# The first LayerNorm's parameters and the constants loaded from ScalarE's queue instead of SyncE's

## The reference, cut to what matters

```python
def layer_norm(x, g, b):
    xf = x.astype(jnp.float32)
    mu = jnp.mean(xf, axis=-1, keepdims=True)
    xc = xf - mu
    var = jnp.mean(xc * xc, axis=-1, keepdims=True)
    return (xc * lax.rsqrt(var + LN_EPS) * g + b).astype(x.dtype)

def reference(x, ln0_g, ln0_b, w_in, ...):
    x = layer_norm(x, ln0_g, ln0_b)
    cos, sin = axial_rope_tables(s, x.dtype)
    for l in range(DEPTH):
        h = x @ w_in[l]
        xf, q, k, v, g_f, g_a = jnp.split(h, SPLITS, axis=-1)
        # Fourier branch, attention branch, gates, output projection
        x = layer_norm(DEEPNORM_ALPHA * x + mixed @ w_out[l], ln1_g[l], ln1_b[l])
        y_p = peer_ffn(x, peer_w_query[l], peer_sub_keys[l], peer_u[l], peer_v[l])
        x = layer_norm(DEEPNORM_ALPHA * x + y_p, ln2_g[l], ln2_b[l])
    return x
```

## Time and profile before

| | us |
|---|---|
| median of 3 runs | 3690.21 (3690.01 to 3690.3) |
| the profiled execution | 3692.19 |
| its span in the trace | 3690.0 |
| PE busy | 3648.8 |
| DVE busy | 2554.0 |
| POOL busy | 2544.3 |
| ACT busy | 1271.2 |

### The profile page before, as it was taken

The page is one execution under the profiler, slowest core; times in us unless marked ns, Lnnn a source line. Parts: engine busy times, 40 slices in busy tenths (PEclk is TensorE's granted clock), DMA queues, the critical chain, the costliest instruction groups (busy, mean ns, idle before and its releaser), DMA issues.

```text
span 3690.0 us, 54294 instructions
## 1 busy us (share of the span) xinstructions
PE 3648.8 (99%) x18216; PEld 3006.1 (81%) x18216; DVE 2554.0 (69%) x4735; ACT 1271.2 (34%) x1859; POOL 2544.3 (69%) x1122
## 2 busy tenths in 40 slices
PE   8999999999999999999999999999999999999998
PEld 7778888888888888888887788888888888888886
DVE  7645979966565656677665469799656565657776
ACT  1651134454344434211126412344444334441110
POOL 6445553349999999877764545533599999998775
PEclk9999999999999999999999999999999999999999
DMA  4223247883333333454321222388634333435542
GB/s 155 69 70 106 100 143 226 244 252 114 125 140 133 114 125 141 178 190 185 137 105 69 80 102 105 138 243 248 212 128 150 120 114 129 150 119 185 202 182 102
DMA packets 221243, 537.87 MB, mean 146 GB/s; under 512 B 9408, under 2 KB 140736, under 8 KB 172864
## 3 DMA queue, kind: packets, MB, share of 16 engines
q1 hardware_dynamic: 47968, 337.14, 25.4%
q10 hardware_dynamic: 173152, 199.13, 16.5%
HBM read 437.67 MB, written 98.57 MB: 145 GB/s over the span
## 4 chain that ended last, share of the span: by engine, by line
PE 95%; DVE 2%; POOL 1%; issue 1%; ACT 0%; DMA 0%; DVEq 0%; POOLq 0%; ACTq 0%
PE bank L1592 30%; PE bank L1593 29%; PE bank L1594 29%; PE bank L1921 2%; PE bank L1922 2%; POOL part_l L529 1%; PE bank L1718 1%; PE bank L1881 1%; PE bank L1706 1%; PE bank L1697 0%; PE bank L1698 0%; POOL part_h L541 0%; DVE stats L1038 0%; DVE bank L1054 0%; PE bank L1670 0%
## 5 line engine op out<-in xcount | busy, mean ns | idle before, releaser
L529 POOL TENSOR_TENSOR part_l<-landing,part_h 128x1024 fp32r<-128x1024 f32 x496 | 1285.7, 2597 | 529.3 <-ACT part_h L806 421.2
L1592 PE MATMUL bank<-XTh,part_h 128*128 128x512 f32 (+1 forms) x2688 | 1047.4, 390 | 3.9 <-DVE XTl L1074 2.5
L1593 PE MATMUL bank<-XTl,part_h 128*128 128x512 f32 (+1 forms) x2688 | 1034.1, 385 | 0.0
L1594 PE MATMUL bank<-XTh,part_l 128*128 128x512 f32 (+1 forms) x2688 | 1034.0, 385 | 0.0
L541 POOL TENSOR_SCALAR part_h<-landing 128x1024 fp32r<-128x1024 f32 x244 | 313.4, 1285 | 497.5 <-PE bank L1594 376.0
L575 POOL TENSOR_TENSOR part_l<-vraw,part_h 128x1024 fp32r<-128x1024 f32 x238 | 596.7, 2531 | 68.4 <-ACT part_h L932 68.4
L1592 PEld LDWEIGHTS bank<-XTh,part_h 128*128 128x128 f32 x2688 | 505.2, 188 | 102.7 <-DVE XTl L1074 3.4
L1594 PEld LDWEIGHTS bank<-XTh,part_l 128*128 128x128 f32 x2688 | 505.1, 188 | 101.3
L1593 PEld LDWEIGHTS bank<-XTl,part_h 128*128 128x128 f32 x2688 | 505.6, 188 | 95.9
L1501 DVE TENSOR_TENSOR X<-X,bank 128x512 f32<-128x512 f32 x544 | 345.0, 680 | 87.3 <-PE bank L1594 87.3
L932 ACT CAST part_h<-vraw 128x1024 fp32r<-128x1024 f32 x238 | 242.1, 1045 | 340.7 <-POOL vraw L582 280.5
(11 more groups left out here) (222 smaller groups left out, 6168.5 us busy)
## 6 DMA issues: line engine op xcount, KB each, us to landing
landing<-stream SPq DMA_DIRECT2D x248, 1024.0 KB, 4.8
vraw<-stream SPq DMA_DIRECT2D x68, 1024.0 KB, 6.5
dense_gates<-spill ACTq DMA_DIRECT2D x32, 2048.0 KB, 9.2
gate<-dense_gates ACTq DMA_DIRECT2D x62, 1024.0 KB, 4.8
early_acts<-early ACTq DMA_DIRECT2D x112, 256.0 KB, 2.2
acts_in<-early_acts ACTq DMA_DIRECT2D x28, 1024.0 KB, 7.5
LNP<-ln ACTq DMA_DIRECT2D x4, 1024.0 KB, 4.8
X<-x SPq DMA_DIRECT2D x4, 512.0 KB, 7.3
```

Source lines behind the costliest of these rows:

```text
L529: nc.gpsimd.tensor_tensor(halves(part_l[s], h), halves(landing[s], h), halves(part_h[s], h).bitcast(F32), ALU.subtract).then_inc(split.sem, 1)
L1592: nc.tensor.matmul(dst, sth, mvh, start=first, stop=False)
L1593: nc.tensor.matmul(dst, sth, mvl, start=False, stop=False)
L1594: return nc.tensor.matmul(dst, stl, mvh, start=False, stop=last)
```

## The change

Two transfers leave SP's queue and are issued by ACT as the first thing in its program, `LNP` before `C`. Their sources, targets and semaphores stay as they were, and so does everything that waits for them. What is left on SP's queue in the beginning is X 0, X 1, `landing[0]`, X 2, X 3, `landing[1]`.

```diff
@@ -443,11 +443,7 @@
             for s in range(LANDINGS):
                 for tb in (2 * s, 2 * s + 1):
                     sp.dma_start(X[:, tb, :], x[tb * P:(tb + 1) * P]).then_inc(x_in[tb], 16)
-                if s == 0:
-                    sp.dma_start(LNP[:], ln0.partition_broadcast(P)).then_inc(ln_in.sem, 16)
                 sp.dma_start(landing[s][:], flat[s]).then_inc(landed[s], 16)
-                if s == 0:
-                    sp.dma_start(C[:], consts).then_inc(const_in, 16)
 
             def rounds(first, end, ahead):
                 with sp.Fori(first, end) as r:
@@ -639,6 +635,8 @@
                     nc.scalar.copy(XTh[:, 4 * h:4 * h + 4, tb * P:(tb + 1) * P],
                                    bank[banks[i]][:].rearrange("p (k t) -> p k t", k=4)).then_inc(xt_high.sem, 1)
 
+            act.dma_start(LNP[:], ln0.partition_broadcast(P)).then_inc(ln_in.sem, 16)
+            act.dma_start(C[:], consts).then_inc(const_in, 16)
             for k in range(2):
                 act.sem_inc(spilled[k].sem, 16)
             root(1, slice(0, 2))
```

## The result

| | before | after |
|---|---|---|
| median of 22 runs, us | 3690.58 | 3695.53 |
| profiled execution, us | 3692.19 | 3696.05 |
| its span, us | 3690.0 | 3694.2 |

The ratio is 1.0014, with a 95% interval of 1.0008 to 1.0020: 5.0 us slower, clear of zero and within the 0.2% that the forecast called no difference. One of the 22 runs of the kernel before took 4818 us; without it the median is 3690.55, and the ratio leaves it out. Lines from 446 on have lower numbers now (1605 is 1603, 1064 is 1062, 1066 is 1064, 1592 is 1590).

What follows compares the result with a forecast made beforehand. PE, busy 3648.8 of 3690.0 us, was taken as the bound, the start being set by DVE's chain to the second pair. That pair's delay, +3.4 to +4.0, taken as +3.7, gave 3690.2+3.7 = 3693.9 us; range 3689.6 to 3696.2.

Steps and rivals of the forecast that it cites:

- no difference: Whole kernel: the forecast shift, +3.7 us, is half of the 0.2% (7.4 us) a measurement can tell; chance of same 0.95.
- pairwise sharing: Start transfers: both queues share by packets, X 0 with LNP, X 1 with C; 3693.9, own range 3692.9 to 3694.9, chance 0.47.
- the signs that the prediction named: X 1 after 8 us, C before 10, DMA wait, four steps over 1.28, second pair at 29 to 31, entry 35.5 to 37.5.
- Issue time is worth nothing: First issues: SP's sooner by 1.1 us or so, ACT's table load moved behind its issues; neither gains anything.
- Order of arrival: Start transfers: X 0 at 7.02, X 1 at 9.50, landing[0] at 11.97; X 1 late by 2.5 to 3.7 us.
- the mild rival: Start transfers: a head start puts X 1 ahead of most of LNP; +2.2 us, 3692.4, chance 0.28.
- Turns with POOL: First pair: all four DVE steps alternate with POOL; fourth ends at 22.95 (POOL first) or 20.9 (DVE first), before 16.54.
- Second pair: DVE's second pair of token blocks: begins at 30.9 with POOL first, 4.0 us later than before; some loss comes back.
- Downstream: From POOL's end and XTl to PE's second half: PE moves as much as these, +3.4 to +4.0 us.
- Carried to the end whole: From 33.38 on PE paces everything, so the start's delay reaches the end in full.
- no effect: Start transfers: engines empty SP's descriptors first, X 0 and X 1 land as before; 0 to +1.5 us, chance 0.16.
- slower beyond 0.2%: Both pairs: X 1 at 9.50 and DVE behind POOL at every turn; +9.2 us, 3699.4, chance 0.04.

Runs made afterwards that it cites:

- e2: Only C moved to ACT's queue, LNP left on SP's, against the kernel before: 3691.64 us, ratio 1.0004.
- e3: Only LNP moved to ACT's queue, C left on SP's, against the kernel before: 3694.17 us, ratio 1.0010.
- e4: Changed kernel with ACT issuing LNP and C only after an added small DVE memset: 3694.63 us, ratio 1.0011 against the kernel before.
- e5: Changed kernel with POOL's first round held until the first pair is normalised: 3696.13 us, ratio 1.0014 against the kernel before.
- e7: Kernel before with the four tensor_scalar steps (part_h) of the first two pieces made by ACT instead of POOL: 3689.94 us, ratio 0.9996.
- e6: Kernel before with C moved ahead of landing[0] in SP's own queue: 3692.46 us, ratio 1.0004.
- e8: Kernel before with C ahead of landing[0] on SP's queue and the first part_h steps by ACT: 3687.59 us, ratio 0.9990.

## Why the prediction was right, and where a term was too small

The measured median, 3695.53, lies in the range, "no difference at 0.2%" holds, and the likeliest case, pairwise sharing, is the one that came. The size was less good: +5.0 instead of +3.7, and 0.6 above that case's own range, which ended at 3694.9. It was the width of the whole range, up to 3696.2, that held it. Of the signs that the prediction named, all came but one: PE's entry is at 38.97, outside of 35.5 to 37.5. Step by step:

- *Issue time is worth nothing.* Right. ACT's table load moved from 0.90 to 1.84, and nobody waited for it.
- *Order of arrival.* Right. 7.02 and 9.50 were worked out for X 0 and X 1, 6.6 and 9.3 came. That both queues get the same number of packets, 4 KB for X and 8 KB for `LNP`, is borne out by the view by queue (34 and 32), though X 0 landed 0.5 ahead of `LNP` and not with it. `landing[0]` 11.97 was worked out, and POOL's start, 12.24, came at 12.22. e2 and e3 give the parts, e4 shows that the mild rival's mechanism, a head start, is real: with 0.9 us of it X 1 landed as if alone. The issues of the change were closer than that.
- *Turns with POOL.* Right, and shown by e5. The fourth step's end was put at 22.95 with POOL first and came at 22.87. The two did ask within 0.02 us (12.20 and 12.22). DVE's row begins first, but it is DVE's step that took 2.14 instead of 1.28 while POOL's took its usual 1.04, so POOL went first; the prediction left that open (DVE first would have given 20.9).
- *Second pair.* Right: 30.9 worked out, 30.82 measured, 3.9 later than before.
- *Downstream.* This is the term that was too small, +3.4 to +4.0 for an entry that moved by 5.6. The prediction followed two paths to the entry. One is DVE's second pair: its last step ends at 32.04 before, and the entry comes 1.3 later (so too in e2, 33.24 and 34.58, and in e7, 30.40 and 31.73). This path moved by 3.9, as worked out. The other is POOL's round: PE's turning of the second pair comes 4.28 after it in the kernel before (26.87 and 31.15), in e2 (28.07 and 32.35), e5 (32.46 and 36.74) and e6 (29.23 and 33.51). It moved by 2.9, also as worked out. Left out was PE's own time. The 48 matmuls of its first half can begin only when the first pair is turned, behind the fourth step, which was now 6.3 later, and they took 12.4 us without a wait: 24.55 to 36.97, where POOL's end would have given 29.7+4.3 = 34.0. The row of the second turning:

```profile
36.97 1.91 PE L1603 MATMUL bank<-C,X 128*128 128x128 f32 x16
```

 The entry is 2.0 behind it, 1.7 later than the 37.3 of DVE's path. Both e3 (23.64 to 35.61) and e4 (23.62 to 35.94) have it too. So the turning is set by the later of POOL's end + 4.3 and PE's first product + its first half, and the entry by the later of the turning + 2.0 and DVE's last step + 1.3. The first half without a wait took 11.8 us in e7, 12.0 in e3, 12.4 here and 12.9 in e8. In the kernel before, it took 12.93, and of these PE waited some 1.1 for POOL, so PE's own path ended at about 30.0 (18.22+11.8), 1.1 ahead of the 31.15: a path that cost nothing there, and whose end moved by 7.0 (its start by 6.3) while the others moved by 2.9 and 3.9. The half differs in length by its first matmuls, which start 0.43 us apart and the later ones 0.23: 3 in the kernel before, 7 in the changed one, 9 in e8, all in stretches whose granted clock reads 1.00. What makes them slow is open. The rivals "no effect" and "slower beyond 0.2%" did not come: `LNP` was not behind the piece, and POOL did not fall further back.
- *Carried to the end whole.* Nearly. Of the entry's 5.6, 5.45 are left at the first product of the second layer (1862.73 before, 1868.18 after). The spans differ by 4.2 only, and that is mostly the profiled execution of before, not the change: at the start of the second layer its matmuls ran slowly for some us. The windows (PE, PEld, DVE, ACT, POOL, clock, DMA, GB/s) just behind that start, before and then after:

```profile
1862.70:1866.20 3.50, 3.47 (x9) 2.69 (x10) 1.76 (x3) 0.00 (x0) 0.00 (x0) 0.54 0.85 306
```

```profile
1868.10:1871.60 3.50, 3.42 (x15) 2.83 (x16) 1.82 (x4) 0.00 (x0) 0.00 (x0) 1.00 0.75 289
```

 Granted clock 0.54, thus nearly all of it at the lower level of 1.2 GHz, and 9 matmuls in 3.5 us instead of 15. Twenty matmuls after the first of the layer, 6.28 us have passed instead of 4.69: 1.6 us lost. e2 and e5 have the same dip in their profiles, the other six do not. That fits the kernel before being recorded at 3692.19 with a median of 3690.58. The prediction took its 2.0 us between the profiled execution and the median for an offset common to both; the changed kernel's is 0.5. Between the entry's 5.6 and the medians' 5.0, 0.6 us stay unexplained.

The rule of the Trainium skill that the prediction cites (DMA: Bandwidth & Descriptors, Queues, rings and completion order), turns packet by packet, held where the issues were together: 34 packets beside 32, and 52 beside 52. In e4 it did not hold between 4 and 6 us, where ACT's queue moved nothing although `LNP` had been issued at 2.07. The measurements decide, and they show both.

## What to carry to other kernels

Moving a transfer to an idle engine's queue does not make it free: at the start of this kernel, where the DMA engines are full, the order in a queue is a priority, and a second queue took half to two thirds of the bytes from what the first had put first. Before moving one, write down when each transfer is needed, and whether anything in front is needed just in time. When a start-up chain is delayed, work out every path that joins at the end of it, also the ones that were a little shorter before; and ask which instructions of two engines will now coincide.

## What was not expected of the hardware

- Two queues that began together shared evenly by packets, and so not by bytes where one has 8 KB and the other 4 KB (34 packets with 0.28 MB beside 32 with 0.13 MB). With 0.9 us between the issues the second queue got nothing until 6 us, almost 4 us after its own issue (X 1 at 5.5, `LNP` at 11.3).
- DVE and POOL asking 0.02 us apart still took turns for the four steps on end, 2.1, 3.2, 2.1, 3.2 us instead of 1.28; here they stayed in step until DVE had no such step left.
- A dip of the granted clock to half for some 3 us came at the same place, the second layer's start, in three of ten profiles and cost 1.6 us there; PE had stood 1.4 us before it in the one shown, but 1.6 us in the changed kernel, which had no dip. What decides is open.
- The first 3 to 9 matmuls behind a turning started 0.43 us apart instead of 0.23 while the granted clock read 1.00. Why is open.
